# A two-block sequence model on one core: a different order of work at the four hand-overs between token-major and feature-major layers

## The reference, cut to what matters

```python
for i in range(2):
    m = mixer_gdn(x, ...) if i == 0 else mixer_gla(x, ...)      # each: x @ w_in ... @ w_out
    x = layernorm(4**0.25 * x + m, ln1_g[i], ln1_b[i])
    h = relu(x @ mlp_w1[i])                                    # 1024 -> 4096
    x = layernorm(4**0.25 * x + (h * h) @ mlp_w2[i], ln2_g[i], ln2_b[i])
# second block
mod = silu(c) @ w_mod + b_mod;  mod_c = silu(c_ctx) @ w_mod + b_mod    # shift, scale, gate
h  = rms(x, norm_g)   * (1 + scale)   + shift
hc = rms(ctx, norm_g) * (1 + scale_c) + shift_c
u, uc = h @ w_in, hc @ w_in      # latent q/k/v, two gates, input of the pooling branch
y = concat(silu(gate_a) * attention(u, uc), silu(gate_p) * pooling(u)) @ w_out
out = x + gate * y
```

## Time and profile before

| | us |
|---|---|
| median of 3 runs (2043.88 to 2045.86) | 2045.12 |
| the profiled execution | 2043.4 |
| its span | 2041.6 |
| PE busy | 1881.9 (92% of the span) |
| DVE busy | 997.9 (49%) |
| ACT busy | 726.0 (36%) |
| POOL busy | 239.4 (12%) |
| hand-over 1 (last tile's product to first slab's end) | 583.9 to 606.7 |
| hand-over 2 | 971.9 to 1006.1 |
| hand-over 3 | 1341.6 to 1364.5 |
| hand-over 4 (last pair's first tile to first product) | 1705.6 to 1758.1 |

### The profile page before, as it was taken

One profiled execution on the slowest core, in us unless ns is written; L12 is line 12 of the kernel. 1 busy time (PEld: TensorE's weight loads), 2 busy tenths in 40 slices (PEclk: granted clock), 3 DMA queues, 4 the chain that ended last, 5 costly groups with the idle time before them and its releaser, 6 DMA issues.

```text
span 2041.6 us, 24057 instructions
## 1 busy us (share of the span) xinstructions
PE 1881.9 (92%) x9070; PEld 1512.0 (74%) x9070; DVE 997.9 (49%) x1408; ACT 726.0 (36%) x1177; POOL 239.4 (12%) x226
## 2 busy tenths in 40 slices
PE   6999999999889999999799888889999998799989
PEld 6887778888668887887577677668887886575667
DVE  2775455555374444445321456464444366513653
ACT  2434544444222223322342343232223334434440
POOL 2001243343000001000000234000000000200410
PEclk8999999999989999999899999989999998899999
DMA  3223100000323324221222100423235231421001
GB/s 123 83 82 103 62 1 1 1 1 1 125 68 96 94 91 137 86 100 62 62 83 83 62 1 1 145 83 103 82 103 180 88 103 42 134 78 62 1 1 62
DMA packets 101442, 146.72 MB, mean 72 GB/s; under 512 B 4673, under 2 KB 70289, under 8 KB 101104
## 3 DMA queue, kind: packets, MB, share of 16 engines
q1 hardware_dynamic: 94272, 119.29, 18.6%
q0 software_dynamic: 6512, 24.20, 3.3%
q10 hardware_dynamic: 576, 2.10, 0.3%
HBM read 143.47 MB, written 2.10 MB: 71 GB/s over the span
## 4 chain that ended last, share of the span: by engine, by line
PE 86%; DVE 7%; ACT 3%; issue 2%; DMA 1%; POOL 1%; ACTq 0%; DVEq 0%; POOLq 0%; SPq 0%
PE bk L261 21%; PE bk L263 21%; PE bk L262 21%; PE bk L953 3%; PE bk L972 2%; PE bk L1711 1%; PE bk L2459 1%; PE bk L2460 1%; PE bk L963 1%; PE bk L2479 1%; ACT whi L246 1%; PE bk L940 1%; DVE wlo L252 1%; PE bk L1075 1%; PE bk L1014 1%
## 5 line engine op out<-in xcount | busy, mean ns | idle before, releaser
L252 DVE TENSOR_TENSOR wlo<-raw,whi 128x1024 fp32r<-128x1024 f32 x224 | 266.5, 1229 | 480.0 <-ACT whi L246 475.6
L261 PE MATMUL bk<-act_hi,whi 128*128 128x512 f32 (+1 forms) x1024 | 412.1, 402 | 7.6 <-DVE act_lo L387 5.0
L262 PE MATMUL bk<-act_lo,whi 128*128 128x512 f32 (+1 forms) x1024 | 409.2, 400 | 0.0
L263 PE MATMUL bk<-act_hi,wlo 128*128 128x512 f32 (+1 forms) x1024 | 409.0, 399 | 0.0
L246 ACT ACTIVATE whi<-raw 128x1024 fp32r<-128x1024 f32 x224 | 226.3, 1052 | 366.0 <-PE bk L263 327.7
L261 PE MATMUL bk<-whi,act_hi 128*128 128x512 f32 x768 | 310.7, 405 | 32.0 <-DVE act_lo L536 17.9
L263 PE MATMUL bk<-whi,act_lo 128*128 128x512 f32 x768 | 310.6, 404 | 0.0
L262 PE MATMUL bk<-wlo,act_hi 128*128 128x512 f32 x768 | 309.0, 402 | 0.0
L261 PEld LDWEIGHTS bk<-act_hi,whi 128*128 128x128 f32 (+1 forms) x1024 | 194.6, 190 | 60.2 <-issue 6.7
L262 PEld LDWEIGHTS bk<-act_lo,whi 128*128 128x128 f32 (+1 forms) x1024 | 194.7, 190 | 48.1 <-issue 0.7
L263 PEld LDWEIGHTS bk<-act_hi,wlo 128*128 128x128 f32 (+1 forms) x1024 | 194.5, 190 | 48.1
(11 more groups left out here) (372 smaller groups left out, 2381.0 us busy)
## 6 DMA issues: line engine op xcount, KB each, us to landing
raw<-in_mlp_w SPq DMA_DIRECT2D x128, 512.0 KB, 4.3
raw<-in_a_w_in SPq DMA_DIRECT2D x32, 512.0 KB, 4.5
work<-in_w_mod POOLq DMA_DIRECT2D x3, 4096.0 KB, 15.9
raw<-in_b_w_in SPq DMA_DIRECT2D x24, 512.0 KB, 3.9
raw<-in_w_in SPq DMA_DIRECT2D x14, 512.0 KB, 4.7
raw<-in_a_w_out SPq DMA_DIRECT2D x8, 512.0 KB, 4.0
raw<-in_b_w_out SPq DMA_DIRECT2D x8, 512.0 KB, 4.0
raw<-in_w_out SPq DMA_DIRECT2D x8, 512.0 KB, 3.9
```

Source lines behind the costliest of these rows:

```text
L252: nc.vector.tensor_tensor(wlo[b][:, hs], raw[hf][:, :], whi[b][:, hs], ALU.subtract).then_inc(w_ready, 1)
L261: nc.tensor.matmul(acc, lhs_hi, rhs_hi, start=first, stop=False, skip_group_check=True)
L262: nc.tensor.matmul(acc, lhs_hi, rhs_lo, start=False, stop=False, skip_group_check=True)
L263: return nc.tensor.matmul(acc, lhs_lo, rhs_hi, start=False, stop=last, skip_group_check=True)
```

## The change

Seven edits.

1. Tile 3 is turned into banks 4 and 5 (`TURN_BANK`), tiles 1 and 2 into 2 and 3. Tile 2 now waits for tile 1's low part, tile 3 for none. At the start the turning of two small tables of vectors waits for the last low part of the input.
2. `pe_feature_first` (hand-overs 1 to 3) multiplies its first feature tile (j = 0) on token tiles 0 to 2, 24 matmuls of 384 columns; then it turns tile 3; then 24 matmuls of 128 columns finish the feature tile; then j = 1 as before.
3. DVE's `split_lo` of the next layer's first slab stands ahead of tile 3's sum, and no longer behind its normalisation.
4. Hand-over 2: the gate projection stands between the two feature tiles of b_qk's first slab; the split of its weights is moved into down0, behind the step that prepares its half-way point.
5. The context is turned in one piece after the first two slabs of down1's second half; ACT and DVE modulate and split it behind the staging of the fifth pair.
6. Hand-over 4: the squares of the normalised tiles are summed by ACT (Square with an accumulated output), not by DVE; the first slab's product waits for feature block 12 of 16 and not for block 13.
7. `pe_c_gate` is moved behind `pe_c_first`; DVE's `dve_c_gate` is moved into `dve_c_in`, behind the splits of two pairs of slabs.

```diff
+        TURN_BANK = (0, 2, 2, 4)
         def pe_turn_tile(pe, e, name, st):
...
-                if st >= 2:
-                    pe.wait_ge(act_ready, 8 * e + 2 * (st - 2) + hf + 1)
+                if st == 2:
+                    pe.wait_ge(act_ready, 8 * e + 2 + hf + 1)
...
         def turn_between(name, e):
             def between(pe, st):
                 if st >= 1:
                     pe_turn_tile(pe, e, name, st - 1)
-                if st == 3:
-                    pe_turn_tile(pe, e, name, 3)
...
             for st in range(1, ST):
+                if st == 3:
+                    split_lo(dve, nxt, 0)
                 dve_norm_tile(dve, name, e, st, lambda: dve_turned(dve, e, st - 1))
-            split_lo(dve, nxt, 0)
             dve_turned(dve, e, 3)
...
+        def pe_feature_first(pe, name, before, e, middle=None):
             pe.wait_ge(w_ready, 2 * (PH[name][0] + 1))
             hi, lo = slab_view(whi[0], KT), slab_view(wlo[0], KT)
+            pe.wait_ge(acc_free, 2 * FS[name] - 3)
+            pe.wait_ge(act_ready, 8 * e + 6)
+            for kt in range(KT):
+                mm3(bk[0][:, 0:3 * P], hi[:, kt, 0:P], lo[:, kt, 0:P], act_hi[:, kt, 0:3 * P], act_lo[:, kt, 0:3 * P], kt == 0, False)
+            pe_turn_tile(pe, e, before, 3)
+            for kt in range(KT):
+                if kt % 4 == 0:
+                    pe.wait_ge(act_ready, 8 * e + 7 + kt // 4)
+                mm = mm3(bk[0][:, 3 * P:S], hi[:, kt, 0:P], lo[:, kt, 0:P], act_hi[:, kt, 3 * P:S], act_lo[:, kt, 3 * P:S],
+                         False, kt == KT - 1)
+            mm.then_inc(acc_ready, 1)
+            if middle is not None:
+                middle(pe)
+            pe.wait_ge(acc_free, 2 * FS[name] - 2)
+            for kt in range(KT):
+                mm = mm3(bk[1][:, :], hi[:, kt, P:2 * P], lo[:, kt, P:2 * P], act_hi[:, kt, :], act_lo[:, kt, :],
+                         kt == 0, kt == KT - 1)
+            mm.then_inc(slab_used, 1)
...
-                act.wait_ge(V.sem, V.at("ms", t))
-                K.inc(nc.scalar.activation(rstd[:, k, 0:1], mv[:, k, 0:1], ACT.Ln, bias=RMS_EPS), "ln")
+                if t < 2:
+                    act.wait_ge(V.sem, V.at("ms", t))
+                else:
+                    act.wait_ge(x_ready, 24 + 2 * n + 2)
+                    K.inc(nc.scalar.activation(dst[:, m, :], src[:, n, :], ACT.Square, accum_out=mv[:, k, 0:1]), "square")
+                    act.wait_ge(K.sem, K.at("square", t - 2))
...
         def dve_c_norm(dve):
             for st in range(ST):
-                dve_norm_tile(dve, "down1", 4, st, lambda: [dve_c_low(dve, i) for i in range(4 * st - 4, 4 * st)] if 0 < st < 3 else None)
-                dve.wait_ge(x_ready, 24 + 2 * st + 2)
-                dve_c_stats(dve, (2 + st,))
-            split_lo(dve, nxt, 0)
+                if st == 3:
+                    split_lo(dve, nxt, 0)
+                dve_norm_tile(dve, "down1", 4, st)
             for i in range(8, 16):
                 dve_c_low(dve, i)
             split_lo(dve, nxt, 1)
+
+        def dve_c_gate(dve):
             dve.wait_ge(T.sem, T.at("gate"))
...
         def pe_c_in(pe):
             pe_c_first(pe)
+            pe_c_gate(pe)
             pe_feature_slab(pe, "c_in", 0, 1)
...
             for b in range(2):
                 split_lo(dve, next_pair("c_in", 1), b)
+            dve_c_gate(dve)
             dve.wait_ge(T.sem, T.at("gst"))
```

More of the change, by code:

```diff
@@ L334, in pe_token_last, with pe_token_layer @@
                 between(pe, st)
-        def pe_token_layer(pe, name, between):
+        def pe_token_layer(pe, name, between, middle=None):
             pairs = PH[name][1] // 4
@@ L344, in pe_token_layer @@
                         pe_token_slab(pe, name, half, 0, b, pair0, b == 0, False)
+                    if half == 1 and middle is not None:
+                        middle(pe)
                     with pe.Fori(1, pairs - 1) as k2:
@@ L486, in act_token_layer @@
                 act_token_steps(act, name, 3, 0)
-                with act.Fori(4, 7) as k2:
-                    act_token_steps(act, name, k2, k2 - 3)
+                if e == 2:
+                    act_b_gate_weights(act)
                 if e == 4:
                     act_c_xn(act, (0, 1))
+                act_token_steps(act, name, 4, 1)
+                if e == 4:
+                    act_c_context(act)
+                with act.Fori(5, 7) as k2:
+                    act_token_steps(act, name, k2, k2 - 3)
             else:
@@ L519, in dve_token_layer @@
             if n > 4:
-                with dve.Fori(4, 7) as k2:
+                if e == 2:
+                    dve_b_gate_weights(dve)
+                dve_token_steps(dve, name, 4, 1)
+                if e == 4:
+                    for i in range(8):
+                        dve_c_low(dve, i)
+                    dve_c_gate_sum(dve, 4)
+                with dve.Fori(5, 7) as k2:
                     dve_token_steps(dve, name, k2, k2 - 3)
@@ L1372, in build, with pe_up @@
         mod_acc = work[:, 8192:10240].rearrange("p (w n) -> p w n", w=2)
[L1374 removed]
+        def pe_up(pe, L, before, e):
             name = f"up{L}"
[L1376 removed]
+            pe_feature_first(pe, name, before, e)
             pe_feature_slab(pe, name, 0, 1)
@@ L1513, in pe_b_in @@
             mm.then_inc(B["gl_mm"], 1)
+        def pe_b_in(pe):
             for k2 in range(2):
                 for b in range(2):
-                    pe_feature_slab(pe, "b_qk", k2, b)
+                    if k2 == 0 and b == 0:
+                        pe_feature_first(pe, "b_qk", "down0", 2, pe_b_low)
+                    else:
+                        pe_feature_slab(pe, "b_qk", k2, b)
                     pe_b_la(pe, 4 * k2 + 2 * b)
@@ L2070, in act_c_high @@
             kt, w = i % 8, 1 if i < 8 else 0
-            act.wait_ge(T.sem, T.at("turned", i))
-            if i >= 2:
+            act.wait_ge(T.sem, T.at("turned", i | 1 if i < 8 else i))
+            if i % 8 >= 2:
                 act.wait_ge(V.sem, V.at("lo", i - 2))
@@ L2076, in act_c_high, with act_c_context @@
             K.inc(nc.scalar.activation(hi, src, ACT.Identity, scale=modg[:, kt, w:w + 1], bias=modc[:, kt, w:w + 1]), "hi")
+        def act_c_context(act):
+            act.wait_ge(V.sem, V.at("ga"))
+            act.wait_ge(stage_ready, STAGED["down1"] + 12)
+            for i in range(8):
+                act_c_high(act, i)
         def act_c_norm(act):
             nxt = next_pair("down1", PH["down1"][1] // 2 - 1)
-            act.wait_ge(V.sem, V.at("ga"))
             for st in range(ST):
                 act_norm_tile(act, 4, st)
-                if st < 2:
-                    for i in range(4 * st, 4 * st + 4):
-                        act_c_high(act, i)
                 if st == 2:
@@ L2102, in pe_c_turn_one, with pe_c_context_turn @@
             T.inc(mm, "turned")
-        def pe_c_context_turn(pe, st):
-            if st == 0:
-                pe.wait_ge(K.sem, K.at("xn", 1))
-                pe.wait_ge(sum_added, 4 * TH["down1"] + 4)
-            if st < 2:
-                for i in range(4 * st, 4 * st + 4):
-                    pe_c_turn_one(pe, i)
+        def pe_c_context_turn(pe):
+            pe.wait_ge(K.sem, K.at("xn", 1))
+            pe.wait_ge(sum_added, 4 * TH["down1"] + 4)
+            for i in range(8):
+                pe_c_turn_one(pe, i)
         def pe_c_turn(pe):
```

59 lines of the change are left out of this document (26 added, 33 removed).

## The result

The changed kernel takes 2031.01 us (median of 4 runs, 2030.55 to 2032.57) where the kernel before takes 2044.5: ratio 0.9934 [0.9917, 0.9952]. A second comparison, on another occasion, gave 2030.01 against 2043.66, ratio 0.9936 [0.9922, 0.9949]. The forecast was 2034.3 in a range of 2026 to 2042, faster with 0.86.

The account below looks back on a forecast made before the run. PE, working 92% of the span, bounds the kernel; gains 3.8 + 7.6 + 0.8 less 1.4 make 10.8 us off the profiled 2043.4, so 2032.6, plus 1.7 for the median: 2034.3. Own range 2029 to 2039; with rivals 2026 to 2042.

Parts of the forecast that it names:

- Hand-overs 1 and 3: PE starts the next layer's first slab on tiles 0 to 2 before tile 3: gain 1.9 us each, bounds 4 and -1.
- the slow stretch: Hand-overs 1 to 3: after PE's stop the clock falls once, in the 384-column pass; price taken as 2.0 us, bounds 0 and 2.7.
- rival E: Hand-overs 1 to 3: clock stays low through the whole first slab, 23.6 us, giving 2058; chance 0.06.
- Hand-over 2: Gate weights split inside down0 remove PE's 8.80 us wait for their low part: gain 7.6 us, bounds 9.6 and 4.
- Hand-over 4: With c_in: earlier turning and product, less transposes, sums, a new stop and slow clock: gain 0.8 us, bounds -2 and +4.
- tiles' ring: Hand-over 4: DVE and ACT alternating set the pace, 6.0 us a tile.
- I take 2.2 here: c_in: price in us of the clock's fall behind PE's 5.3 us stop for the gate's bias addition.
- Start: Tile 2's first half waits for tile 1's low part, and table transposes follow: loss 1.4 us, bounds 0.5 and 2.
- B: Clock does not fall in the first feature tiles or behind the gate's wait: 8 us more gain, 2026; chance 0.1.
- C: Hand-overs 1 to 3: 128-column matmuls run at quarter rate, 8.4 us less gain, 2043 at the worst; chance 0.12.
- D: c_in: the gate's wait does not bind, PE being held elsewhere; 5.3 + 2.2 us back, 2027; chance 0.05.
- F: down1: the context's steps make ACT and DVE late for the sixth pair, 2 to 5 us, 2038; chance 0.12.

Follow-up runs that it names:

- e1: Changed kernel with DVE's gate bias additions moved ahead of the splits of c_in's third pair of slabs: 2022.92 us, ratio 0.9902 to the kernel before.
- e6: Changed kernel with the squares' sums on VectorE again in place of ScalarE's Square: 2037.17 us, ratio 0.9971 to the kernel before.
- e11: Changed kernel with the gate's weights rounded behind hand-over 2 again: 2026.39 us, ratio 0.9932 to the kernel before.
- e4: Changed kernel with PE's stop at hand-overs 1 to 3 filled by 24 matmuls of 256 columns, result overwritten: 2028.70 us, ratio 0.9928 to the kernel before.
- e5: Changed kernel with tile 3 turned inside the 384-column pass, ahead of its block 5: 2022.38 us, ratio 0.9906 to the kernel before.
- e8: Changed kernel with earlier gate additions, gate sums ahead of hand-over 4's turning, filled stops, tile 3 turned inside the 384-column pass: 2014.61 us, ratio 0.9861.
- e10: Changed kernel with earlier gate additions, filled stops at hand-overs 1 to 3, tile 3 turned inside the 384-column pass: 2019.51 us, ratio 0.9886.
- e9: Changed kernel with the context's turning and steps back between hand-over 4's tiles, four blocks behind each of the first two: 2042.55 us, ratio 0.9997.

## Why the prediction was right

**Hand-overs 1 and 3: mechanism right, 1.0 us too high.** First product 4.24 us behind tile 2's turning (predicted 4.35), turning with its hand-offs 2.02 (2.05), narrow matmuls 0.114 each (0.11), slow clock in the first pass 1.6 (2.0). The step that failed is "the slow stretch" in the singular: a second fall behind the narrow matmuls costs 1.5 us. It was a part of rival E, at 3 x 1.5 instead of 3 x 6.4. Where it stays away (e1, e6, e11) the gain is 2.4 us, above the forecast.
The Trainium skill, "TensorE: Matmul & The Clock Gate", section "Back-to-back issue gap", would have had the narrow matmuls at 81 ns; 24 took 2.7 us at full clock, so the measurement decides for 0.114.
The Trainium skill, same page, section "Part 4: PE-mode transpose", spoke for E, as transposes do not count as PE work for the clock there. The runs bear it out in part at most: behind the turning in the middle with its stop a second fall came at 11 of 21 places, but at none of the 12 where the stop ahead was filled, matmuls stood on both sides of the turning, or both (e4, e5, e8, e10).

**Hand-over 2: right in size (6.8 for 7.6), wrong in its reason.** The same second fall, 1.5 us, is more than the difference. "The gate's weights are split inside down0, so the 8.80 us wait goes" is true, but e11 shows that it goes without that as well. The prediction counted one wait for one edit; the chain behind it, the load that waits for the split, was named at hand-over 1 and not followed here.

**Hand-over 4: predicted 0.8, measured 3.2.** The tiles' ring is 5.94 us (6.0), the turning, counted from the hand-over's beginning, 10.65 us earlier (9.95), block 12 brings 1.84 (1.95), the sums cost 1.88 (1.8), the stop 5.32 (5.3), the context in down1 1.9 (1.8). The term that failed is the clock, "I take 2.2 here": the slow stretch behind the stop came as said, but the kernel before had one behind its own first product (1759 to 1762), and that one went (windows of PE, the kernel before and the changed one):

```profile
1758.00:1763.00 5.00, 4.92 (x15) 0.66 0.26 82
```

```profile
1738.00:1743.00 5.00, 4.93 (x21) 1.00 0.00 0
```

Stop and sums take 7.2 of the 7.4 us by which the c_in span grew; so the net price of the clock was 0.2, not 2.2. I charged the new fall, which e1 prices at 1.9, and did not look for the old one that goes. What makes the old one go is not isolated; in e6 and e9, whose stops before the turning are 14.36 and 17.38 us where the changed kernel's is 10.50, it is there.

**Start.** -0.3 instead of -1.4. 0.4 of the difference is the input, which landed at 15.51 instead of 15.88; counted from there the first product came 0.7 us later (8.83 for 8.14 us). The stop was 0.65 us, not 1.0, and it did not pass on whole: counted from the input, PE was released by the last low part only 0.3 us later than before (8.42 for 8.14 us). The tables' transposes behind it took 0.4 as said.

**The rivals.** B: refused, the clock fell at hand-overs 1 to 3 and behind the gate's wait. C: refused, the narrow matmuls follow each other in 0.114 us and not in 0.23. D: refused by the stop, and e1 shows what it was worth, 7.2 us. F: no stop of PE at the sixth pair. E: partly, above.
The sum was off by only 1.8 us because the errors (-2.8 at hand-overs 1 to 3, +2.4 at hand-over 4, +1.1 at the start, +1.1 in unchanged code) nearly cancel. That is luck, and so is a part of the last term. The median is 3.3 us under the forecast and not 1.8, because the 1.7 us added for the median over the profiled execution were not there: the changed kernel's profiled execution is within 0.2 us of its median.

## What to carry to other kernels

- A wait that is put down to one instruction may belong to the queue ahead of it. Before an edit is credited with such a wait, look at what the instruction stood behind; two edits on the same chain are worth little more than one.
- When an operation is moved along an engine's queue, ask for each thing that it is now behind when that can start. Here an addition of 1.3 us, moved behind a split that had to wait for the very slab in front of the waiting matmul, cost 7.2 us, more than half of what the change gained.
- A stop of PE costs its length and then the clock. Count falls on both sides of a change, the old one that goes as well as the new one, and expect that a part of a removed fall comes back in unchanged code.

## What the runs showed of the hardware

- With a stop of 3.2 us filled with matmuls the clock was 1.00 through the 4 us of 384-column matmuls behind it (9 of 9 places in e4, e8 and e10). Unfilled, it fell behind that stop at 23 of 24 places (0.53 over 3.5 us at hand-over 1) and stayed at 1.00 at one (e5, hand-over 2).
- The same instructions, with the same stops to 0.01 us, had the second fall in one execution and not in another; it differs even between the three hand-overs of one execution.
- ScalarE's Square of 128 x 1024 with its sum takes 1.06 us and 0.19 for reading out the sum, 1.18 us from its start to the next instruction's; a scaling of the same size takes 1.15 us (1.06 to the next), VectorE's statistics for it 1.70 us to the next (e6).
- A matmul of 128 columns follows the last in 0.114 us, one of 384 in 0.173 to 0.175 at full clock and 0.32 at half.
